# Expert matrices as one 16 KB run per partition, token rows gathered whole into half of the partitions

## The reference, cut to what matters

```python
def hier_moe(x, w_rg, w_re, w1, w3, w2):      # x: 512 tokens x 1024
    g_prob = softmax(x @ w_rg); g_gate, g_idx = top_k(g_prob, 1)     # 1 of 4 groups
    e_w, e_i = top_k(softmax(logits of the 8 experts of the group), 2)
    weights = g_gate * e_w / sum(e_w)
    for each expert e, for the tokens xb that chose it:
        hdn = silu(xb @ w1[e]) * (xb @ w3[e])  # w1, w3: 1024 x 512
        out[token] += weight * (hdn @ w2[e])   # w2: 512 x 1024
```

## Time and profile before

| | us |
|---|---|
| median of 3 runs | 1874.71 (1871.57 to 1875.13) |
| the profiled execution | 1872.44 |
| its span, first to last instruction | 1870.6 |
| PE busy, share of the span | 1769.5, 95% |
| DVE, ACT, POOL busy | 756.5, 543.4, 153.9 |

### The profile page before, as it was taken

The page is one execution under the profiler, slowest core; times in us unless marked ns, Lnnn a source line. Parts: engine busy times, 40 slices in busy tenths (PEclk is TensorE's granted clock), DMA queues, the critical chain, the costliest instruction groups (busy, mean ns, idle before and its releaser), DMA issues. The chain is left out here.

```text
span 1870.6 us, 24010 instructions
## 1 busy us (share of the span) xinstructions
PE 1769.5 (95%) x9586; PEld 986.1 (53%) x9586; DVE 756.5 (40%) x1469; ACT 543.4 (29%) x1117; POOL 153.9 (8%) x194
## 2 busy tenths in 40 slices
PE   8999888989889999999999999899999999999998
PEld 3333455455444444555564444577645544577763
DVE  2244478142511211233224124677424337466642
ACT  2111378123100101333224111454312242344420
POOL 2110001001111111110100014000000003000000
PEclk9999999999999999999999999999999999999999
DMA  7655858448999999999870231000200012000001
GB/s 272 225 195 180 131 135 74 160 165 345 420 418 417 416 416 417 419 417 415 354 295 18 72 129 51 1 1 1 105 0 35 23 62 89 2 1 1 1 24 45
DMA packets 92047, 324.81 MB, mean 174 GB/s; under 512 B 12296, under 2 KB 28808, under 8 KB 64928
## 3 DMA queue, kind: packets, MB, share of 16 engines
q1 hardware_dynamic: 78080, 302.55, 44.4%
q10 hardware_dynamic: 8656, 12.32, 1.9%
q0 software_dynamic: 5200, 8.41, 1.2%
HBM read 317.58 MB, written 14.30 MB: 177 GB/s over the span
## 5 line engine op out<-in xcount | busy, mean ns | idle before, releaser
L1057 PE MATMUL mix_ps<-arena 128*64 128x256 f32 x2048 | 237.0, 384 | 12.7 <-DMA arena<-in_w 5.1
L2129 PE MATMUL tail_ps<-arena 128*128 128x512 f32 x504 | 219.8, 592 | 0.8 <-DMA arena<-in_w_plg 0.8
L1057 PEld LDWEIGHTS mix_ps<-arena 128*64 128x64 f32 x2048 | 144.7, 138 | 98.3 <-issue 25.7
L945 PE MATMUL mix_ps<-arena,side 128*128 128x512 f32 x384 | 175.6, 610 | 1.4 <-DVE side L1411 1.4
L461 DVE TENSOR_REDUCE tail_small<-tail_ps 128x1 f32<-128x768 f32 x128 | 116.6, 953 | 117.2 <-PE tail_ps L337 117.2
L2129 PEld LDWEIGHTS tail_ps<-arena 128*128 128x128 f32 x504 | 94.9, 190 | 115.3 <-issue 114.9
L1069 PE MATMUL mix_ps<-arena 128*64 128x512 f32 x512 | 120.3, 613 | 21.5 <-DMA arena<-in_w 21.0
L945 PEld LDWEIGHTS mix_ps<-arena,side 128*128 128x128 f32 x384 | 72.3, 194 | 103.0 <-issue 84.8
L2129 PE MATMUL tail_ps<-arena,side 128*128 128x512 f32 (+2 forms) x320 | 119.6, 534 | 0.0
L551 ACT ACTIVATE arena<-tail_ps,tail_small 128x768 f32<-128x768 f32 x128 | 113.7, 898 | 3.7 <-DVE tail_small L461 3.7
L337 PE MATMUL tail_ps<-side,arena 96*128 96x512 f32 (+1 forms) x256 | 92.1, 504 | 6.4 <-ACT arena L551 5.8
(11 more groups left out here) (384 smaller groups left out, 2328.7 us busy)
## 6 DMA issues: line engine op xcount, KB each, us to landing
arena<-in_w SPq DMA_DIRECT2D x96, 2048.0 KB, 21.8
arena<-in_l_w_mod SPq DMA_DIRECT2D x16, 1024.0 KB, 5.0
arena<-in_l_w_in SPq DMA_DIRECT2D x16, 1024.0 KB, 7.0
arena<-in_w_in SPq DMA_DIRECT2D x12, 1024.0 KB, 9.2
arena<-in_l_w_mod SPq DMA_DIRECT2D x16, 512.0 KB, 4.6
residual<-bias_blocks SPq DMA_DIRECT2D x32, 224.0 KB, 11.6
arena<-in_l_w_in ACTq DMA_DIRECT2D x12, 512.0 KB, 11.0
arena<-in_l_w_out SPq DMA_DIRECT2D x6, 1024.0 KB, 5.1
```

The costliest lines, as they stand in the source:

```text
L945: last = pe.matmul(ps[:, u % 4], oT[:, k, t * P:(t + 1) * P], weights.slot(W_IN[n, k // 4], 4, 512)[:, k % 4], start=(k == 0), stop=(k == ...
L1057: last = pe.matmul(out[h * CAP:(h + 1) * CAP, 0:H2], x, wb[:, k, h * H2:(h + 1) * H2], start=(k == 0), stop=(k == DK - 1))
L2129: last = pe.matmul(out, lhs(k), rhs(k), start=(k == 0), stop=(k == K - 1))
```

## The change

It has four parts that hang together.

- **Loads.** Partition p now holds rows 8p to 8p+7 of w1 or w3, and 4p to 4p+3 of w2. That is one run of 16 KB instead of two of 8 KB. The bytes, the slots and the order stay.
- **Gathers.** A row of 1024 is gathered whole (4 KB) into one partition. Only 64 partitions receive, and the buffers of even and odd experts are the lower and the upper 64 partitions. The indices are those of tokens, without the doubling and the half; the DVE instruction that makes them has a constant in place of `spare_row`.
- **Turning.** The rows are turned with 8 transposes, each 64 rows by 128 columns with a step of 8 elements, in place of 4 of 128 by 128 with a step of 4. The results fill the same 512 columns of `px`, and the gain is multiplied in by one instruction over the same number of elements.
- **First products.** The hidden columns of the two halves of the array alternate in pairs (columns 0, 1, 4, 5, ... and 2, 3, 6, 7, ...), so that the hidden values come out in the order of the new w2 rows. The number and sizes of the matmuls stay. The moving operand is read as pairs with a step of four.

In the loop at the end the same is done, and PE waits for `x_taken` before `got` and adds one semaphore increment.

```diff
-        read_row=f(2 * token - 4 * SEQ),
+        read_row=f(token - 4 * SEQ),
...
-        g_ffn_x=np.asarray(a["g_ffn"]).reshape(2, P, 4).transpose(1, 0, 2).reshape(P, 8)
+        g_ffn_x=np.asarray(a["g_ffn"]).reshape(P, DK)
...
-    xg, xT = view(work, 0, 2, 512), view(work, 1024, 4, P)
+    xg, xT = [view(work, 0, D)[b * CAP:(b + 1) * CAP] for b in range(2)], view(work, 1024, DK, CAP)
...
-                sp.dma_start(runs(matrix_at[q % 5]), A[which][e].rearrange("(a p j) n -> p a (j n)", a=2, p=P)).then_inc(s["w"][q % 5], 16)
+                sp.dma_start(matrix_at[q % 5], A[which][e].rearrange("(p j) n -> p (j n)", p=P)).then_inc(s["w"][q % 5], 16)
...
-            def turn_rows(buf, sem, n, done):
+            def turn_runs(b):
+                ident = m["ident"][b * CAP:(b + 1) * CAP, b * CAP:(b + 1) * CAP]
+                for j in range(DK):
+                    last = pe.transpose(px[:, j * CAP:(j + 1) * CAP], xg[b].rearrange("p (c j) -> p j c", j=DK)[:, j], ident)
+                return last
+
+            def turn_rows(b, sem, n, done):
                 pe.wait_ge(sem, n)
-                for j in range(4):
-                    last = pe.transpose(px[:, j * P:(j + 1) * P], buf.rearrange("p (c j) -> p j c", j=4)[:, j], m["ident"])
-                last.then_inc(done, 1)
+                turn_runs(b).then_inc(done, 1)
...
             def first_product(out, wb):
                 for k in range(DK):
-                    x = xT[:, k % 4, (k // 4) * CAP:(k // 4 + 1) * CAP]
+                    cols = wb[:, k].rearrange("p (q h j) -> p h q j", h=2, j=2)
                     for h in range(2):
-                        last = pe.matmul(out[h * CAP:(h + 1) * CAP, 0:H2], x, wb[:, k, h * H2:(h + 1) * H2], start=(k == 0), stop=(k == DK - 1))
+                        last = pe.matmul(out[h * CAP:(h + 1) * CAP, 0:H2], xT[:, k], cols[:, h], start=(k == 0), stop=(k == DK - 1))
...
             with pe.Fori(0, pe.value_load(trips_over, min_val=1, max_val=OVER + 1)) as i:
+                pe.wait_ge(s["x_taken"], STATIC)
                 pe.wait_ge(d["got"], 16 * i + 16)
-                pe.wait_ge(s["x_taken"], STATIC)
-                for j in range(4):
...
+                pe.sem_inc(d["go"], 1)
+                turn_runs(p).then_inc(d["turned"], 1)
...
             def gather(e):
-                pool.indirect_dma_start(out=xg[:, e % 2], out_offset=None, in_=x_rows,
-                                        in_offset=bass.IndirectOffsetOnAxis(ap=index[:, 0, e:e + 1], axis=0), **rows_read).then_inc(s["got"][e % 2], 16)
+                pool.indirect_dma_start(out=xg[e % 2], out_offset=None, in_=xn,
+                                        in_offset=bass.IndirectOffsetOnAxis(ap=index[0:CAP, 0, e:e + 1], axis=0), **rows_read).then_inc(s["got"][e % 2], 16)
```

More of the change, by code:

```diff
@@ L126, in parameters @@
     return pack(dict(
-        g_ffn=columns(a["g_ffn"]), g_ffn_x=np.asarray(a["g_ffn"]).reshape(2, P, 4).transpose(1, 0, 2).reshape(P, 8), g_plg=columns(a["g_plg"]),
+        g_ffn=columns(a["g_ffn"]), g_ffn_x=np.asarray(a["g_ffn"]).reshape(P, DK), g_plg=columns(a["g_plg"]),
         l0_norm=columns(a["l0_norm_2"]), l1_norm=columns(a["l1_norm_2"]),
@@ L699, in first_layer @@
     ss_c, sd_c, rs_c, half_c = (view(small, 716 + 2 * k, CT) for k in range(4))
-    xg, xT, yb = view(work, 0, 2, 512), view(work, 1024, 4, P), view(work, 1536, 2, 512)
+    xg, xT, yb = [view(work, 0, D)[b * CAP:(b + 1) * CAP] for b in range(2)], view(work, 1024, DK, CAP), view(work, 1536, 2, 512)
     sact, hid, hT = view(work, 2560, 256), view(work, 2816, 256), view(work, 3072, 2, P)
@@ L707, in first_layer @@
     ys = nc.dram_tensor("expert_out", [2 * SEQ + CAP, D], F32).ap()
-    x_rows, y_rows = (v.rearrange("t (a d) -> (t a) d", a=2) for v in (xn, ys))
+    y_rows = ys.rearrange("t (a d) -> (t a) d", a=2)
     px, p1, p3, ph, py = (ps[:, b] for b in range(5))
@@ L896, in _ @@
                     sp.wait_ge(d[done], FIRST + i)
-                    sp.dma_start(runs(to), A[which][ds(e, 1)].rearrange("x (a p j) n -> p (x a) (j n)", a=2, p=P)).then_inc(d[which], 16)
+                    sp.dma_start(to, A[which][ds(e, 1)].rearrange("x (p j) n -> p (x j n)", p=P)).then_inc(d[which], 16)
             src_c = A["l0_w_in"].rearrange("(k p) n -> p k n", p=P)
@@ L1574, in _ @@
             dve.wait_ge(s["listed"], 1)
-            chain(dve.tensor_tensor(slot_rows, ps[:, 4, 0:N_EXPERTS], m["spare_row"].to_broadcast([P, N_EXPERTS]), ALU.add))
+            chain(dve.tensor_scalar(slot_rows, ps[:, 4, 0:N_EXPERTS], 4.0 * SEQ, None, ALU.add))
             dve.tensor_copy(index[:, 0], slot_rows).then_inc(s["indexed"], 1)
@@ L1638, in overflow_listed @@
                 chain(dve.tensor_copy(gate_w2[:, 0:1], gate_w[:, STATIC:STATIC + 1]))
-                chain(dve.tensor_tensor(over[:, 0:OVER], told_row(0), m["spare_row"].to_broadcast([P, OVER]), ALU.add))
+                chain(dve.tensor_scalar(over[:, 0:OVER], told_row(0), 4.0 * SEQ, None, ALU.add))
                 chain(dve.tensor_copy(index_over[:, 0, 1:OVER + 1], over[:, 0:OVER]))
@@ L1833, in _ @@
                     else:
[L1834 to L1835 removed]
+                        pool.indirect_dma_start(out=xg[STATIC % 2], out_offset=None, in_=xn,
+                                                in_offset=bass.IndirectOffsetOnAxis(ap=index[0:CAP, 0, STATIC:STATIC + 1], axis=0), **rows_read).then_inc(d["got"], 16)
                 if e:
@@ L1847, in _ @@
                 pool.sem_inc(d["go"], 1)
-                pool.indirect_dma_start(out=xg[:, STATIC % 2], out_offset=None, in_=x_rows,
-                                        in_offset=bass.IndirectOffsetOnAxis(ap=current[:, 0:1], axis=0), **rows_read).then_inc(d["got"], 16)
+                pool.indirect_dma_start(out=xg[STATIC % 2], out_offset=None, in_=xn,
+                                        in_offset=bass.IndirectOffsetOnAxis(ap=current[0:CAP, 0:1], axis=0), **rows_read).then_inc(d["got"], 16)
                 pool.wait_ge(d["y_out"], FIRST + i + 1)
```

12 lines of the change are left out of this document (4 added, 8 removed).

## The result

The change made the kernel slower: 1889.13 us median of 6 runs, the kernel before beside it 1873.22 of 6, ratio 1.0089 with a 95% interval of 1.0071 to 1.0106. The forecast was 1874.1, and the measured time lies above the upper end of its 8 in 10 range, 1881.5. The profiled execution has a span of 1888.0 us against 1870.6, so 17.4 us more, and they can be placed.

A forecast was written before the change was run, and what follows sets the result against it. Transfers were taken to bound the kernel to 751 us, PE from there to 910. Loads -5.0, turning +4.3, start +0.4, end -0.3 sum to -0.6 us: forecast 1874.1, own range 1871 to 1877, 8 in 10 range 1868.5 to 1881.5.

The forecast's parts named there:

- Rival A: Gathers into 64 partitions load half of the engines, each expert costing 0.33 us more; in all +5.6, 1880.3; chance 0.22.
- Loads, -5.0: Transfer-bound stretch to 751 us: one 16 KB run saves 87 ns a load, over 57 loads -5.0 us.
- Turning, +4.3: PE-bound stretch, 751 to 910 us: four more transposes at 0.12 us, 0.48 per expert, nine turnings, +4.3 us.
- The cover up to 751 us: Until 751 us the turning's extra 0.48 us per expert disappears in PE's idle time; without that cover 9.6 us.
- First products, 0: Moving columns read as pairs don't lengthen the first products' pace: 0 us.
- Rival E: Pairs slow the first products by a factor 1.46; about +91 us, 1966; decides from 6% on; chance 0.05.
- Start, +0.4: First expert: gather lands 0.3 us earlier, its turning takes 0.7 longer, moving the transfers' whole chain: +0.4 us.
- End, -0.3: From 910 us on, the loop's turning goes into PE's wait for w2; four loads save 0.087 each: -0.3 us.
- B: Early start: first gather lands 2.2 us earlier and PE's shorter idle time keeps its clock; 1870.0; chance 0.10.
- C: Short moving operands: eight transposes take no longer than four; -4.3 and -0.7, 1869.1; chance 0.12.
- D: Loads' runs are cut at 8 KB, or memory is slower at the wider step; +5.3, 1879.4; chance 0.08.
- F: Each transpose waits for its whole weight load; +6.6 and the start's share, about +7, 1881.4; chance 0.05.

The follow-up runs named there:

- pair gather: Kernel after, but the rows of two experts come in one gather of 128 partitions by 4,096 bytes: 1877.07 us, ratio 1.0015 to the kernel before.
- the last run: Whole change without its gathers and turning: gathers into 128 partitions, four transposes, 16 KB loads, pairs of columns, ScalarE storing permuted rows: 1873.05 us, ratio 0.9988.
- the one with 64 partitions on the kernel before: Kernel before, each gather filling only the lower 64 partitions with the lower half of each token's row, upper halves left out: 1874.31 us, ratio 1.0007.
- the one with wide gathers of halves: Kernel after with the gathers of before into 128 partitions, rows turned by 16 products of 64 by 64 with the identity: 1893.91 us, ratio 1.0108.

## Why the prediction was wrong

**The step that failed** is the first sentence on the gathers: "The bytes are the same. Each gather is issued about two rounds before it is used, so only the first one shows." In the kernel after no turning waited for a gather but the first, so that part held. But the engines that carry them are the ones that set the pace, and what a transfer does to the others on these engines was not asked. The runs showed in its place: a gather into 64 partitions lengthens the loads' packets while it moves, and costs 13 to 14 us. An estimate by the packets: 27 ns more for each 16 KB packet (645 - 618), 8 on an engine for a load and 3 loads a round, are 0.65 us, with the gather's own packets (2 on an engine, 44 ns more each) 0.74 us a round, and over 20 rounds 15 us. Measured, the pair gather took back 13.1, and the wide gathers of the last run 14.3.

**Rival A** pointed at the right place, the half of the partitions, with a wrong mechanism and a size that was too small (+5.6). It had a 64-partition gather fall on half of the engines. By the chains above it is the other way round: the gather of 64 partitions spreads over all 16, the one of 128 with the same live rows over about half, and it is the spreading one that disturbs. The trace of before could not show this, for it has no transfer of that shape. But A counted only the gather's own bytes, and every load in flight is touched, so that its +5.6 us fell short of the real 13 to 14.

**Loads, -5.0:** right in kind. The packets number 65,792 against 78,080 in q1 with the same 302.55 MB, the median of 16 KB is 616 ns, and alone the edit gave 3.6 us of the 5.0 in the stretch up to round 20.

**Turning, +4.3:** the mechanism was right, the price too high: 0.34 us instead of 0.48 for each expert, +3.1. The pace was that of the rows: in the kernel after the first four of a turning took 0.65 us and all eight 1.09, so 0.11 for one more:

```profile
617.54 0.65 PE L1048 MATMUL mix_ps<-first,arena 64*128 64x64 f32 x4
```

What the sum had missed is that a group of the smaller ones starts from less, 0.65 us for four against the 0.75 of before. The cover up to 751 us held: in the run with pair gathers the turning's extra time was there and the stretch was down at 328.6.

**First products, 0:** wrong. Reading the moving operand in pairs of float32 cost 4.6% (3.67 to 3.84 us). Rival E had the mechanism and the factor 1.46; the real one is 1.046, under the 6% from which E would decide, but it adds 3.3 us on PE's stretch. The Trainium skill (Advanced Engine Details and Errata, SBUF Cachelines), by which two hits on a line give full speed, is not borne out: 32 instructions took 3.84 us against 3.67 in the run where only this was changed. Why is not shown.

**Start, +0.4:** the sum had -0.3 for the gather and +0.7 for the turning. Measured: +1.1 for the gather, which landed after 8.2 us, and nothing for the turning, 1.12 us against 1.10. What made that gather later is not settled: PE waited 4.70 and 4.80 us for it in two runs with loads of 16 KB and the old gathers, 4.76 in the one with 64 partitions on the kernel before, 5.06 before, and 5.6 to 6.1 in all that were built on the kernel after, the one with wide gathers of halves too (5.74). So the width alone does not do it.

**End, -0.3:** L1072 waits 0.66 us for w2 in the loop, where L1069 waited 1.16; the loop's turning went into that wait, as said. From the loop's turning to this product it is 11.1 us before and 11.3 after, so the 0.3 can't be seen.

With the measured prices the sum is -3.6 + 13.1 + 3.1 + 3.3 + 1.1 = +17 us. The medians differ by 15.9. This is no check from outside, since 13.1 is read against the same profile of the kernel after, and that profile's 17.4 hold 2.55 us of an earlier start and 1.7 at the end, which are chance. **Rivals B, C, D and F** are out: the granted clock was 0.50 again from 420 to 425 us, eight transposes took longer than four, the long runs weren't cut, and no transpose waited for a whole weight load (1.09 us, not 1.69).

## What to carry to other kernels

Where the DMA engines set the pace, ask of every side transfer not only how many bytes it moves and whether it is early, but whether it has the shape of the transfers that it shares the engines with: a gather of 64 partitions beside loads of 128 cost about 0.7 us a round for 128 KB (13 to 14 us in 20 rounds), and the same rows in gathers of 128 partitions next to nothing. If two consumers can share a gather, fill all partitions. And where a layout for one operand asks for another order in the other, look for an instruction that is writing that data anyway: the permuted store had no price that shows (1.148 us for a copy, as before), while pairs in the moving operand and small transposes had.

## What was not expected of the hardware

- A 64-partition indirect gather lengthens the packets of the loads while it moves: in the kernel after 16 KB packets take 759 ns on average beside it and 614 beside the scatter of 128 partitions, 8 KB packets 398 and 312 with the loads put back, and its own packets 204 where the scatter's take 159. A 128-partition gather has little of this (16 KB packets 625 beside it and 614 beside the scatter, with the loads alone changed), even if half of its rows are out of range (8 KB packets: 322 and 312).
- Pairs of float32, 8 bytes out of every 16, as moving operand: 4.6% slower.
- A ScalarE copy of 128 x 1024 float32 that permutes columns in groups of four took 1.148 us, as the dense one.
- Eight transposes with 64 moving columns took 1.09 us, 1.5 times the 0.75 of four with 128.
